# A hybrid decoder step on one core: eight items of a written-out plan change places, and ScalarE's queue stores two halves of an output

## The reference

```
hn = rmsnorm(h, norm_mix);  z, xbc, dt, q, k, v = split(hn @ w_in)
y_ssd: causal conv, then a scan over states (prompt in 2 chunks of 128; samples from state_ssm)
y_att: block-sparse attention; samples over 8 cached pages of 128 keys each (cache_k, cache_v)
h += concat(y_ssd, y_att) @ w_out
h += attention(rmsnorm(h, norm_ca) @ w_ca_q, memory keys and values) @ w_ca_o
h += relu(rmsnorm(h, norm_mlp) @ w_up)^2 @ w_down
y = rmsnorm(h, norm_final);  also returned: k, v, memory k, v, conv and scan states
```

## Time and profile before

| | |
|---|---|
| median of 3 runs | 650.11 us (649.38 to 651.97) |
| profiled execution | 650.07 us, its span 648.4 us |
| PE busy | 629.1 us, 97% |
| DVE, ACT, POOL busy | 405.7, 152.3, 139.0 us |
| mean granted PE clock | 0.997 |
| DMA | 125.75 MB, mean 194 GB/s |

### The profile page before, as it was taken

The page is one execution under the profiler, slowest core; times in us unless marked ns, Lnnn a source line. Parts: engine busy times, 40 slices in busy tenths (PEclk is TensorE's granted clock), DMA queues, the critical chain, the costliest instruction groups (busy, mean ns, idle before and its releaser), DMA issues.

```text
span 648.4 us, 13116 instructions
## 1 busy us (share of the span) xinstructions
PE 629.1 (97%) x4877; PEld 504.6 (78%) x4877; DVE 405.7 (63%) x879; ACT 152.3 (23%) x409; POOL 139.0 (21%) x222
## 2 busy tenths in 40 slices
PE   8999999999999999999999999999999999999995
PEld 6766776676676655557667876899999999999995
DVE  3466576997764667777423346887887874553733
ACT  3110020001212875783102333211211110000001
POOL 6152212110220026151001100433443540000000
PEclk9999999999999999999999999999999999999998
DMA  8798998897942158878696551344544535534501
GB/s 311 242 295 258 290 295 262 243 289 243 286 134 66 66 194 249 311 184 248 199 324 233 210 194 66 112 149 131 171 155 138 187 132 183 176 131 150 172 5 74
DMA packets 98779, 125.75 MB, mean 194 GB/s; under 512 B 6571, under 2 KB 74687, under 8 KB 98722
## 3 DMA queue, kind: packets, MB, share of 16 engines
q1 hardware_dynamic: 92818, 106.62, 50.9%
q0 software_dynamic: 5648, 18.14, 8.9%
q10 hardware_dynamic: 256, 0.20, 0.1%
HBM read 116.64 MB, written 8.31 MB: 193 GB/s over the span
## 4 chain that ended last, share of the span: by engine, by line
PE 77%; DVE 3%; ACT 1%; issue 1%; DVEq 0%; ACTq 0%
PE ps L1618 34%; PE ps L1194 25%; PE ps L1151 4%; PE ps L1261 3%; PE ps L1427 1%; PE ps L1214 1%; PE ps L1373 1%; PE ps L1309 1%; PE ps L1157 1%; PE ps L1303 1%; PE ps L1285 1%; PE ps L1417 1%; PE ps L1406 1%; PE ps L1236 1%; PE ps L1292 1%
## 5 line engine op out<-in xcount | busy, mean ns | idle before, releaser
L1194 PE MATMUL ps<-hw,wring 128*128 128x288 f32 x576 | 148.4, 413 | 0.4 <-DVE big L2126 0.4
L1194 PEld LDWEIGHTS ps<-hw,wring 128*128 128x128 f32 x576 | 108.1, 192 | 37.3 <-issue 6.9
L2253 DVE STREAM_TRANSPOSE tmp<-big 128x1024 f32<-128x1024 f32 x32 | 37.9, 1222 | 2.5 <-PE ps L1214 2.4
L1005 POOL TENSOR_TENSOR acc<-acc,sq 128x288 f32<-128x288 f32 (+1 forms) x35 | 29.3, 836 | 31.5 <-ACT sq L1842 29.3
L2099 DVE COPY tmp<-ps 128x512 f32<-128x512 f32 (+6 forms) x35 | 21.5, 619 | 21.3 <-PE ps L1151 16.0
L1618 PE MATMUL ps<-hw,wring 128*128 128x144 f32 x256 | 34.2, 287 | 0.0
L1618 PE MATMUL ps<-big,wring 128*128 128x144 f32 x256 | 34.0, 286 | 0.0
L1618 PEld LDWEIGHTS ps<-hw,wring 128*128 128x128 f32 x256 | 32.5, 190 | 0.4 <-DVE hw L2103 0.4
L1194 PE MATMUL ps<-big,wring 128*128 128x288 f32 x128 | 32.7, 409 | 0.0
L1194 PE MATMUL ps<-attT,wring 128*128 128x288 f32 x128 | 31.9, 407 | 0.7 <-DVE hT L2148 0.7
L1618 PEld LDWEIGHTS ps<-big,wring 128*128 128x128 f32 x256 | 32.4, 190 | 0.0
(11 more groups left out here) (352 smaller groups left out, 1150.9 us busy)
## 6 DMA issues: line engine op xcount, KB each, us to landing
wring<-in_w_in SPq DMA_DIRECT2D x16, 1024.0 KB, 7.1
wring<-in_w_up SPq DMA_DIRECT2D x16, 1024.0 KB, 5.1
wring<-in_w_down SPq DMA_DIRECT2D x16, 1024.0 KB, 4.7
big<-in_cache_v SPq DMA_DIRECT2D x56, 256.0 KB, 3.5
big<-in_cache_k SPq DMA_DIRECT2D x36, 256.0 KB, 3.5
big<-in_cache_k POOLq DMA_DIRECT2D x28, 256.0 KB, 4.2
wring<-in_w_out SPq DMA_DIRECT2D x6, 1024.0 KB, 5.8
wring<-in_w_ca_kv SPq DMA_DIRECT2D x4, 1024.0 KB, 8.2
```

What stands on the lines that cost most here:

```text
L1005: pool.tensor_tensor(a, a, sq[:, m % 2, 0:n], ALU.add).then_inc(acc_done, 1)
L1194: last = pe.matmul(ps[:, BANK[key], 0:width], w, rhs, start=(k == 0), stop=(k == K_TILES[kind] - 1))
L2253: dve.transpose(KT_[:, step_ % 2].rearrange("p c (w j) -> p w c j", j=32), src[:, :, :, m, :])\
```

## The change

`norm_mix` is loaded ahead of `x_sample` on ACT's queue. `qrep` moves behind the tile (qk, 2, 0). `norm 0` moves behind `mtok` and `hist`. `kvtok 0 2` is split in two, and the second half moves behind `seg 0 3`. The value unit (0, 2) moves from behind `yo 1 1` to ahead of `seg 1 0`. The memory key turns `mkt 0 n` come ahead of the tiles `oa n` instead of behind them, but for the last. The two stores of rows 128 to 255 of `y_prompt` go from SP's queue to ACT's. No arithmetic changes.

```diff
-    def keys(group, k, kind, n, between=None):
+    def keys(group, k, kind, n, *between):
         item("kt", group, k, 0)
         tile(kind, n, 0)
-        if between:
-            seq.append(between)
+        seq.extend(between)
         item("ks", group, k, 0)
...
-    item("qrep")
-    keys(0, 0, "qk", 2, ("ss", "mem"))
+    keys(0, 0, "qk", 2, ("qrep",), ("ss", "mem"))
...
-    item("norm", 0)
     item("mtok")
     item("hist")
+    item("norm", 0)
     keys(1, 1, "x", 0)
...
-    item("kvtok", 0, 2)
+    item("kvtok", 0, 1)
     item("yo", 0, 0)
     item("seg", 0, 2)
     item("yo", 0, 1)
     item("seg", 0, 3)
+    item("kvtok", 1, 2)
     item("yo", 0, 2)
...
     item("sums", 1)
+    unit("V", 0, 2)
     item("seg", 1, 0)
     item("seg", 1, 1)
     item("yo", 1, 0)
     item("seg", 1, 2)
     item("yo", 1, 1)
-    unit("V", 0, 2)
     item("zsq", 0)
...
     for n in range(4):
+        if n != 3:
+            item("mkt", 0, n)
         pair("oa", n)
-        item("mkt", 0, n)
+    item("mkt", 0, 3)
     unit("MK", 0)
...
                 sp.dma_start(O["y_prompt"][0:P, cols], yrow[0][:, cols]).then_inc(y_out, 16)
-                sp.wait_ge(y_act, i + 1)
-                sp.dma_start(O["y_prompt"][P:2 * P, cols], yrow[1][:, cols]).then_inc(y_out, 16)
...
             act.dma_start(ident[:, :], I["ident"]).then_inc(ident_in, 16)
+            act.dma_start(vec_rows[0:DT, :], I["norm_mix"].rearrange("(r n) -> r n", n=P)).then_inc(mix_in, 16)
             for i in range(2):
                 cols = slice(512 * i, 512 * i + 512)
                 act.dma_start(xin[0:NS, 2, cols], I["x_sample"][:, cols]).then_inc(x_in[i], 16)
-                if i == 0:
-                    act.dma_start(vec_rows[0:DT, :], I["norm_mix"].rearrange("(r n) -> r n", n=P)).then_inc(mix_in, 16)
...
                 act.activation(y, y, ACT.Copy, scale=finv[:, 1:2]).then_inc(y_act, 1)
+                act.wait_ge(y_act, i + 1)
+                act.dma_start(O["y_prompt"][P:2 * P, 512 * i:512 * i + 512], y).then_inc(y_out, 16)
```

## The result

The changed kernel takes **654.04 us** (median of 10 executions, 651.20 to 656.50) against 649.75 for the kernel before on the same chip (10 executions, 648.64 to 652.27). The ratio is 1.0066 [1.0042, 1.0090]: 0.66% slower. That is 2.4 us above the forecast of 651.6 and above its own range (to 653.0), inside the whole range (to 654.4), on the side to which the text had given 0.20, and nearest to the rival in which the clock falls (654.6). Against the kernel before it is +4.3, where +1.5 was forecast.

A forecast was written before the change was run, and what follows sets the result against it. TensorE (PE) was taken to bound the kernel nearly everywhere. Terms -0.3 - 0.7 + 1.1 + 2.6 - 0.7 - 0.5 = +1.5 on 650.07 gave 651.6 us; own range 650.4 to 653.0, 8 in 10 between 647.0 and 654.4.

The forecast's parts named there:

- the rival in which the clock falls: Behind PE's 4.6 us wait for the value load, matmuls run partly at half clock: 3 more, 654.6 us; chance 0.17.
- first vector: At the start, loading `norm_mix` ahead of `x_sample` shortens PE's wait before the x transposes: -0.3 us.
- `qrep`: Near 35 us, running it behind tile (qk, 2, 0) removes PE's 1.50 wait and starts key steps earlier: -0.7 us.
- `norm 0`: Near 109 us, DVE's work behind the history copies delays the block transposes PE waits for: +1.1 us.
- split and value unit, stall: Near 263 us, PE reaches the value unit 4.6 us before its load lands, delaying the scan's last output: +2.6 us.
- memory keys: Near 344 us, memory key transposes fill PE's 0.69 wait before the first `oa` tile: -0.7 us.
- stores: At the end, two stores on ACT's queue let the last store issue earlier: -0.5 us, bounds -0.8 and 0.
- ACT becomes the longer chain: Behind the value unit, ACT's exponentials, squares and scalings put the last output 11.0 us after the unit's end.
- The 0.7 of the split is swallowed too: Splitting `kvtok` brings PE 0.7 us earlier to the end of the sums, but the value load's wait takes that.
- the same 2.84 behind the last issue: At the end, the span still ends 2.84 us after the last store's issue, so it moves from 648.4 to 647.9.

The follow-up runs named there:

- the three good moves together: The kernel before with only `qrep`, the memory keys and the split `kvtok` changed, value unit in its old place: 648.86 us, ratio 0.9964.

## Why the prediction was right and where it was not

| step | predicted | shown |
|---|---|---|
| first vector | -0.3 | +0.1 (alone: 0.0) |
| `qrep` | -0.7 | -1.0 |
| `norm 0` | +1.1 | +1.1 |
| split and value unit, stall | +2.6 | +2.4 |
| clock behind the stall | 0 (a rival, +3) | +2.4 |
| memory keys | -0.7 | -0.9 |
| stores | -0.5 | +0.6 |
| sum | +1.5 | +4.8 |

The right column is read from the profiled execution at the places listed above and its sum is made before rounding: it is that execution's 6.5 less the 1.7 at 222. The medians differ by 4.3. The +0.1 at the start is that execution's own: other executions of the same load order were 0.1 to 4.2 ahead there. The waits listed in the first paragraph of the prediction add up to 12.4 and not to 12.1; nothing hangs on it.

- **The stall** was priced rightly, in its parts: load issued at 259.4 and landed 9.7 later (9.8 before), a wait of 4.70 (4.6), and 12.99 from the unit's start to the last output where the clock holds (12.9). The reason given for the last was not right: "ACT becomes the longer chain" isn't seen. Behind the unit PE has a single gap, 0.39 before the last output, so the 11 us are PE's own work. "The 0.7 of the split is swallowed too" held; the split brings 1.1, and with the unit in its old place it is kept. The prediction looked only at the 0.83 before the last output of chunk 0, which fell to 0.33; the split also removed a wait of 0.56 that the kernel before had at 253.43 for DVE's eviction.
- **The step that failed is the base rate of "The clock falls"**, which got a chance of 0.17 and left the forecast's sum without a clock term. The text argued that the clock fell when PE ran out of work, that no wait of before was over 1.5 and this one would be 4.6, and then took the high clock anyway. It read the fall off the 40 slices of the page alone. Stretches of 2 us show it in the kernel before: PE's last matmul ended at 641.5, and the clock fell just before 645, with PE idle in between. The new wait would be 4.6 long:

```profile
642.00:644.00 2.00, 0.00 (x0) 0.00 (x0) 1.60 (x7) 1.52 (x6) 0.00 (x0) 1.00 0.00 0
644.00:646.00 2.00, 0.00 (x0) 0.00 (x0) 0.69 (x2) 0.49 (x1) 0.00 (x0) 0.74 0.76 294
```

  The rival gave 3 us, for about a quarter of 11 us at the low level; the runs gave 2.4 in the changed kernel and 1.9 to 2.6 over three executions with waits over 4 us, and none when the wait was filled. The Trainium skill (TensorE: Matmul & The Clock Gate, The HAM clock gate) says that idling halves TensorE's clock, and this case's rows agree: granted 0.50 in each of the three executions with an empty wait of over 4 us, and no fall behind those of 0.2 and 0.54. By that rule the forecast would have been 651.6 plus the 3 priced there: 654.6, against 654.04 measured.
- **The stores**: the step set the end by "the same 2.84 behind the last issue". The last issue moved as said, but that distance was SP's, with transfers whose medians were 2.4 and 2.5; with ACT's queue beside it they were 2.5, 3.0 and 3.3. The bounds were -0.8 and 0, so the true value lay outside. No row of before showed ACT's queue at that load, which should have put the upper bound above 0.
- **The first vector**: "the wait only passes from `norm_mix` to `x_sample`" was named as a bound and is what happened.
- `qrep`, `norm 0` and the memory keys came out within 0.3 of their numbers, each by the wait and the releaser named.

What the time hid: the good edits are worth 3.0 us together in the trace (1.0, 0.9 and 1.1), and this was less than one stall.

What stays open: why the clock drops for some 3.4 us near 222 and 246 in some executions, with PE busy throughout. It is worth about 1.7 us each time, and with the start, worth up to 4, it may make up much of the spread of all these kernels. And how much of the changed kernel's spread (651.2 to 656.5) is due to the stall's clock was not separated. The mean clock doesn't tell: its two fastest executions had 0.991 and the slowest 0.98, but the one profiled again had 0.991 too, at 655.02.

## What to carry to other kernels

A long wait of TensorE for a load has two prices: the wait, and matmuls at half the clock behind it. Read the landing time of the load (issue plus the row's time to landing) before putting its user anywhere, put the user at the first place behind it, and add the clock's price for a long empty wait (here it fell in each of over 4 us, in one of 2.06 perhaps by chance, and, once the first 20 us are over, behind none of up to 1.5). If no work can fill the wait, matmuls whose results are thrown away can. At the start of this kernel two of them were worth about as much (3.0 us by means) as the three good moves together (2.2).

## What the runs showed of the hardware

- In the three executions with a wait over 4 us the clock fell during the wait, not behind it: in the changed kernel PE stopped at 264.39, and the stretch from 266 to 268 already had 0.83. It stayed low for 3.6 to 5 us of the work behind. With the unit alone moved, PE stopped at 266.1 and started again at 268.14, and the clock fell at 269.3.
- At the start a granted clock of 1.00 in the record can't be trusted. In the kernel before it reads 1.00 in each stretch from 0 to 22 us, but the same 24 transposes take 6.95 there and 4.41 elsewhere, and the first 20 records of matmuls on ones take 4.64 (0.23 each), where 40 of them at 258 took 4.63 (0.12 each). The durations, not the record, show the half rate. Where the record has 0.50 at the start, the durations agree: in the changed kernel it falls at 7.9, 1.2 us behind a wait of 1.29, is low until 18.1, and the first tile takes 6.75. Seven executions show such a fall, between 7.9 and 10.3, behind waits of 0.55 to 1.29. No wait of up to 1.5 does this later in the kernel, and the cause is open.
- Low stretches also come in the midst of full work: in the changed kernel the tile at 222.56 took 5.83, most of it at 0.50.
- With two of the last five stores on ACT's queue, all of the last transfers took longer (2.5, 3.0 and 3.3 us by group, against 2.4 to 2.5 all on SP's), although they were issued over a shorter time. In the changed kernel they moved some 400 GB/s until 652.5 and 160 to 270 in the 1.5 us behind that; in the kernel before it was 356 to 414 from 644.5 to 647.5, when they were through.
